# Modulation sums moved out of the feed-forward layers into the mixers of a fused transformer kernel

## The chip, the cores and the metric

The kernel runs as one program on one core of a Trainium2 chip. The metric is the device time of one execution in microseconds (us), the median of several runs. Of the core's engines, TensorE (PE) does the matmuls and writes PSUM, VectorE (DVE) and ScalarE (ACT) do the elementwise work, GpSimd (POOL) does a little, and SyncE (SP) issues most of the loads from HBM. ACT and POOL can issue loads too. Each engine works through its own list of instructions in order, and a wait on a semaphore holds everything behind it on that engine.

## The reference

Two blocks are computed one after the other on 256 tokens of width 1024, each with two layers, all in float32. A layer is a mixer (several kinds of token mixing side by side, then an output projection) and a feed-forward. The first block has one dense feed-forward and one with 8 experts, the second block has two dense ones. What matters here is the second block's modulation: a vector of 6 x 1024 numbers for each layer, from one conditioning vector `c`:

```python
c_act = jax.nn.silu(c)
for l in range(DEPTH):                                   # DEPTH = 2
    mod = (c_act @ ada_w[l] + ada_b[l])[:, None, :]      # ada_w[l]: 1024 x 6144
    sh1, sc1, g1, sh2, sc2, g2 = jnp.split(mod, 6, axis=-1)
    h = rmsnorm(x, norm_mix_g[l]) * (1.0 + sc1) + sh1
    ...                                                  # mixer, x = x + g1 * (mix @ w_out[l])
    h = rmsnorm(x, norm_ffn_g[l]) * (1.0 + sc2) + sh2
    f = (jax.nn.silu(h @ ffn_w1[l]) * (h @ ffn_w3[l])) @ ffn_w2[l]
    x = x + g2 * f
```

`mod` depends on nothing but the inputs, so it can be computed at any time before the layer that uses it.

## The kernel before, in words

The stages run in this order. First block: mixer 0 ("mix0"), dense feed-forward "ffn0", a gated projection "ple0", mixer 1 ("mix1"), the experts, "ple1". Second block: mixer "mixb0", feed-forward "ffnb0", mixer "mixb1", feed-forward "ffnb1", the final norm.

The order on every engine is written out by hand. Functions such as `dve_ff`, `act_mixers1` or `pe_mixers2` list the instructions of one engine for one stage, and every helper waits on named signals (`wait_ge`) and raises its own (`then_inc`). There is no scheduler. All compute instructions are issued in one helper line, which is why the profile gives L91 for nearly all of them, and L115 for the loads; they are told apart by engine and tile.

**The modulation sums.** `ada_w` comes as 48 chunks for each layer, each 128 rows by 1024 columns (512 KB). One DVE instruction (`dve_ada_sum`) multiplies a chunk by the replicated `c_act` (`c_row`) and sums along the row into one column of the tile `mods` ("modulation"). The chunk is loaded from the ACT queue (`act_ada_load`), each into one of four places of the big tile `ring`. The load into a place waits for the sum that read this place last (`adasum{n-4}`). The 48 chunks for layer 0 of the second block are all summed inside ffn0, and the 48 of layer 1 all inside ffnb0. Inside ffnb1 there are none. Both ffn0 and ffnb0 also load `c` and take its silu on ACT, at their start (`act_ada_start`).

**A feed-forward layer** has 22 blocks of 128 hidden columns, in 11 pairs. Pair 0 is done by plain matmuls (`pe_ff_up`). Pairs 1 to 10 use a Strassen-like scheme of seven products instead of eight (`pe_ff_pair`). For each of them DVE makes sums of weights for the next pair (`dve_ff_w`, 4 pieces), and puts the products together (`dve_ff_c11`, `dve_ff_c22`, `dve_ff_c12`, `dve_ff_pair_hid`); ACT copies one product and takes the silu. I call this the up stage. Then comes the down stage: 11 pairs of hidden blocks times the down weights, seven products of 128x512 each (`pe_ff_down`, n = 1, 2, 6, 5, 3, 7, 4), added up in seven PSUM banks. Product 6 of pair p waits for DVE: for the sums of hidden values (`dve_ff_hid_sums`, four instructions of 128x128) and of weights (`dve_ff_down_sums`, four of 128x512). PE runs pairs 0 to 7 one after the other, and the last three product by product, so that product 6 of pair 10 is its 65th of 77. At the end `dve_ff_close` adds the totals to the residual.

In `dve_ff` the modulation sums stand between these instructions: three in each of the pairs 1 to 10 of the up stage, one after it, and then one or two after each `dve_ff_down_sums`.

**The mixers.** PE goes through column tiles of the input projection (`pe_win`, 384 columns for 128 tokens at a time), ACT copies each result out of PSUM (`act_z`, written `z(t, i)`), and the next tile of the same half of the tokens waits for this copy. Between the tiles PE does the small matmuls of the mixing, in step with DVE and ACT. In mix1 DVE has nothing to do from the normalisation until `dve_rw_mix`, which needs the third tile, and then waits again before `dve_rw_wa`. In mixb0 it waits before `dve_cf_gate`, which starts a long chain of convolution taps, and again before the residual is added. The copies `act_rw_lo_copy` (mix1) and `act_cf_turn` (mixb0) stand between a turn on PE and what follows on PE or DVE.

SP loads the weights of the next stage into slots of `ring` as these come free. Some of those loads wait for the last modulation sum of the layer (`ada_done`).

Of the kernel before, what the change touches and what calls it, by code (L numbers as in the profile page):

```python
# [16 lines left out]
P = 128  # L17
# [218 lines left out]
def build(nc, d):  # L236
# [26 lines left out]
    mods = sb("modulation", 2 * 48 + 16)  # L263
    posi = nc.alloc_sbuf_tensor("posi", [P, 2 * NT], I32)[:, :]
# [1177 lines left out]
    SUMS_AT, TSUMS_AT, CGATE_AT, ADA_AT = (30720, 27648), 24576, 26624, (4096, 22528, 23552, 11264)  # L1442
    xs = xn_flat.rearrange("p (k t) -> p k t", k=KD)
    x_sums = flat[:, TSUMS_AT:TSUMS_AT + 2048].rearrange("p (e k t) -> p e k t", e=4, k=4)
    c_row = flat[:, CGATE_AT:CGATE_AT + D]
    ff_kept = xt_flat[:, 0:512]
    ADA_COLS = 48

# [323 lines left out]
    def act_ff(s, ada, l=None):  # L1772
        if ada is not None:
            act_ada_start(s, ada)
# [31 lines left out]
    def act_ada_load(s, ada, n):
        if n > 3:
            act.wait_ge(f"{s}.adasum{n - 4}")
        act.load(ada_place(n), d["ada"][ada, n], f"ada{n % 4}", f"{s}.ada{n}")

    def dve_ada_sum(s, ada, n):
# [3 lines left out]
        dve.wait_ge(f"{s}.ada{n}", f"{s}.crow")
        at = ADA_COLS * ada + n
        dve(V.scalar_tensor_tensor, out=ada_place(n), in0=ada_place(n), scalar=1.0, in1=c_row, op0=ALU.mult, op1=ALU.mult,
            accum_out=mods[:, at:at + 1]).then_inc(f"{s}.adasum{n}")

    def dve_ff(s, ada):  # L1820
        taken = iter(range(ADA_COLS if ada is not None else 0))

        def ada_sum():
            for n in itertools.islice(taken, 1):
                dve_ada_sum(s, ada, n)
# [11 lines left out]
        for p in range(1, NPAIR):  # L1837
# [5 lines left out]
            ada_sum()  # L1843
# [2351 lines left out]
```

## Time and profile before

| | us |
|---|---|
| runs | 2135.66, 2132.59, 2134.96 |
| median | 2134.96 |
| profiled execution, device time | 2133.81 |
| its span, first to last instruction | 2132.4 |
| PE busy in it | 2028.9 (95%) |
| DVE busy in it | 975.9 (46%) |
| ACT busy in it | 415.8 (20%) |

The granted TensorE clock is 0.983 of full speed over the span. The slices of the page show DVE at 8 or 9 tenths in two stretches only, which are ffn0 (about 206 to 438 us) and ffnb0 (about 1554 to 1788 us); in ffnb1 (about 1916 to 2121 us) it is at 6 or 7. PE is at 9 tenths nearly everywhere, and at 7 to 8 in some slices, two of which are the ends of ffn0 and ffnb0. A span counts as PE busy from the start of a matmul to its modelled end, so a PE that runs at half its clock also reads as busy.

### The profile page before, as it was taken

The page shows a single profiled execution, that of the slowest core. Times are in us where ns is not written, and L with a number is a line of the kernel's source. Part 1 is how long each engine was busy: PE and PEld are TensorE (multiplying, and loading weights), DVE is VectorE, ACT ScalarE, POOL GpSimd, SP SyncE. Part 2 cuts the span into 40 slices and gives each one's busy share as a digit, 9 for nine tenths or more (in the row PEclk, how much of TensorE's full clock was granted, in tenths as well). Part 3 has the DMA queues.
Part 4 walks back from the last instruction along what each step waited for, and adds up shares of the span by engine and source line. Part 5 has one row for each costly group of instructions (what it writes and reads, how often), then busy time and mean ns, then how long its engine had stood idle before and what let it go on. Part 6 is the DMA issues. An engine that isn't in the chain of part 4 may idle for free.

```text
span 2132.4 us, 31502 instructions
## 1 busy us (share of the span) xinstructions
PE 2028.9 (95%) x13197; PEld 1201.6 (56%) x13197; DVE 975.9 (46%) x1755; ACT 415.8 (20%) x918; POOL 60.8 (3%) x63
## 2 busy tenths in 40 slices
PE   8979999799988999999999999999999997999997
PEld 5665996365764433322333233366689834669973
DVE  2664899832773100000000000146579995747676
ACT  2454000031453000000101001052420002331001
POOL 0021000000110000000000000100000000000000
PEclk9999999899999999999999999999999999999999
DMA  6222977433233999999999999823378853435430
GB/s 236 92 111 117 364 289 271 150 153 118 82 130 127 405 423 414 416 424 410 423 412 424 424 424 424 356 112 139 138 296 299 295 166 131 159 139 231 174 139 30
DMA packets 70758, 536.54 MB, mean 252 GB/s; under 512 B 10129, under 2 KB 10641, under 8 KB 28529
## 3 DMA queue, kind: packets, MB, share of 16 engines
q1 hardware_dynamic: 53824, 474.28, 55.5%
q10 hardware_dynamic: 14112, 51.39, 6.8%
q0 software_dynamic: 2672, 8.78, 1.1%
q8 instruction: 107, 1.75, 0.3%
q14 instruction: 43, 0.34, 0.0%
HBM read 528.77 MB, written 7.75 MB: 252 GB/s over the span
## 4 chain that ended last, share of the span: by engine, by line
PE 67%; DVE 22%; DMA 6%; ACT 3%; issue 2%; DVEq 0%; SPq 0%; ACTq 0%
PE ps L91 67%; DVE ring L91 17%; DMA ring<-in_moe 6%; DVE transposed L91 2%; ACT ring L91 2%; DVE stat L91 1%; DVE natural L91 1%; DVE z L91 1%; ACT natural L91 1%; DVE gates L91 0%; DMA ring<-in_c 0%; DVE residual L91 0%; DVEq L75 0%; ACT L91 0%; ACT z L91 0%
## 5 line engine op out<-in xcount | busy, mean ns | idle before, releaser
L91 PE MATMUL ps<-ring 128*32 128x512 f32 (+8 forms) x5968 | 890.5, 446 | 62.8 <-DVE ring L91 45.0
L91 PEld LDWEIGHTS ps<-ring 128*128 128x128 f32 (+4 forms) x5968 | 472.0, 153 | 417.1 <-issue 335.1
L91 PE MATMUL ps<-ring,transposed 128*128 128x384 f32 (+4 forms) x1408 | 469.3, 489 | 3.3 <-ACT transposed L91 2.0
L91 PEld LDWEIGHTS ps<-ring,transposed 128*128 128x128 f32 x1408 | 259.4, 190 | 185.2 <-issue 62.2
L91 PE MATMUL ps<-ring,z 128*32 128x512 f32 (+4 forms) x1718 | 327.3, 581 | 0.3 <-ACT z L91 0.3
L91 DVE TENSOR_TENSOR z<-z,ps 128x256 f32<-128x256 f32 (+4 forms) x80 | 34.6, 433 | 622.9 <-ACT z L91 601.7
L91 DVE TENSOR_TENSOR ring<-ring 128x512 f32<-128x512 f32 (+3 forms) x320 | 275.8, 862 | 17.7 <-ACT ring L91 0.8
L91 PEld LDWEIGHTS ps<-ring,z 128*32 128x32 f32 (+3 forms) x1718 | 110.6, 129 | 195.5 <-issue 193.2
L91 DVE SCALAR_TENSOR_TENSOR ring<-ring 128x256 f32<-128x256 f32 (+3 forms) x222 | 177.0, 797 | 14.6
L91 PE MATMUL ps<-natural,ring 128*128 128x128 f32 (+1 forms) x1472 | 174.7, 275 | 1.4 <-ACT natural L91 0.8
L91 PEld LDWEIGHTS ps<-natural,ring 128*128 128x128 f32 x1472 | 169.5, 192 | 2.4 <-issue 1.2
L91 ACT COPY z<-ps 128x256 f32<-128x256 f32 (+6 forms) x112 | 46.9, 419 | 508.8 <-PE ps L91 508.1
L91 DVE TENSOR_TENSOR transposed<-transposed,ps 128x512 f32<-128x512 f32 (+1 forms) x120 | 74.5, 621 | 44.5 <-PE ps L91 36.2
L91 ACT ACTIVATE z<-transposed 128x512 f32<-128x512 f32 x30 | 18.9, 630 | 347.7 <-DVE transposed L91 347.7
L91 ACT ACT_TABLE_LOAD x59 | 75.7, 1283 | 16.1 <-issue 12.4
L91 ACT ACTIVATE z<-ps 128x256 f32<-128x256 f32 (+2 forms) x67 | 25.0, 373 | 215.3 <-PE ps L91 209.8
L91 ACT COPY transposed<-ps 128x256 f32<-128x256 f32 (+1 forms) x55 | 23.3, 424 | 188.9 <-PE ps L91 185.9
L91 ACT COPY ring<-ps 128x512 f32<-128x512 f32 (+4 forms) x80 | 41.5, 518 | 77.9 <-PE ps L91 74.8
L91 ACT ACTIVATE natural<-residual 128x512 f32<-128x512 f32 (+2 forms) x52 | 31.0, 597 | 123.4 <-DVE residual L91 115.5
L91 PEld LDWEIGHTS ps<-constants,z 128*128 128x128 f32 (+1 forms) x263 | 26.8, 146 | 49.8 <-issue 46.4
L91 ACT ACTIVATE z<-ps,stat 128x384 f32<-128x384 f32 (+2 forms) x44 | 24.4, 554 | 123.8 <-PE ps L91 122.7
L91 PE MATMUL ps<-transposed,ring 128*128 128x257 f32 (+2 forms) x208 | 43.8, 380 | 1.3 <-DVE transposed L91 1.3
(159 smaller groups left out, 1024.4 us busy)
## 6 DMA issues: line engine op xcount, KB each, us to landing
ring<-in_moe SPq DMA_DIRECT2D x87, 2048.0 KB, 20.1
ring<-in_moe SPq DMA_DIRECT2D x90, 1024.0 KB, 18.7
ring<-in_ffn_up SPq DMA_DIRECT2D x66, 1024.0 KB, 7.1
ring<-in_ada ACTq DMA_DIRECT2D x96, 512.0 KB, 4.4
ring<-in_w_in SPq DMA_DIRECT2D x25, 1536.0 KB, 6.4
ring<-in_ffn_down SPq DMA_DIRECT2D x33, 1024.0 KB, 7.2
ring<-in_w_out SPq DMA_DIRECT2D x12, 1536.0 KB, 7.1
ring<-in_ple_gate SPq DMA_DIRECT2D x4, 1536.0 KB, 11.8
```

Source lines behind the costliest of these rows:

```text
L91: self.ins = None if self.book.counting else op(*args, **kw)
```

## The change

The 96 sums and the 96 chunk loads stay. Their places change:

- A tile of its own, `ada_mem` ("ada_chunks", 3 x 1024 columns), holds two chunks and `c_row`. `c` is loaded and its silu taken once, in ffn0. The room in SBUF comes from a smaller scratch for GpSimd's DMA descriptors (`dynamic_dma_scratch_size=4096`).
- 33 of the 48 sums of layer 0 stay in ffn0. 15 go to mix1: 11 ahead of `dve_rw_mix` ("mix") and 4 ahead of `dve_rw_wa` ("wa"). 34 of layer 1 stay in ffnb0. 14 go to mixb0 ("mixb"): 9 ahead of `dve_cf_gate` and 5 ahead of the residual.
- In the up stage a pair has 3 or 2 sums in turn (`ADA_PAIRS`, 25 in all), in the down stage there is one for each pair (8 in ffn0, 9 in ffnb0).
- The sums and weights for down pair 0 (`dve_ff_hid_sums(s, 0)`, `dve_ff_down_sums(s, 0)`) are one step earlier on DVE, in all three dense layers.
- The loads go round over six places in the feed-forward, three in mix1 (two own ones and the end of `zbuf`), two for "wa", and five in mixb0. They are issued by ACT between its copies `z(t, i)`. A load waits for the sum that read the place before it.

```diff
+    ada_mem = sb("ada_chunks", 3 * D)
...
-    c_row = flat[:, CGATE_AT:CGATE_AT + D]
+    c_row = ada_mem[:, 2 * D:3 * D]
+    ADA_TURNS = {"ff": ("own0", "own1", "ring0", "ring1", "ring2", "ring3"), "mix": ("own0", "own1", "z"), "wa": ("own0", "own1"),
+                 "mixb": ("own0", "own1", "sums0", "sums1", "sums2")}
+    ADA_PAIRS = (3, 2, 3, 2, 3, 2, 3, 2, 3, 2)
+    ADA_PARTS = ([(0, "ff", sum(ADA_PAIRS) + 8), (0, "mix", 11), (0, "wa", 4)],
+                 [(1, "mixb", 14), (1, "ff", sum(ADA_PAIRS) + 9)])
...
     def act_ada_start(s, ada):
         act.part("ada")
         act.wait_ge(f"{s}.xt10", f"{s}.xt11")
-        act.load(c_row, d["c"].to_broadcast([P, D]), "c", f"{s}.c")
-        for n in range(4):
-            act_ada_load(s, ada, n)
-        act.wait_ge(f"{s}.c")
-        act(S.activation, c_row, c_row, ACT.Silu).then_inc(f"{s}.crow")
...
+        if ada == 0:
+            act.load(c_row, d["c"].to_broadcast([P, D]), "c", "ada.c")
+        for n in ada_of[ada, "ff"][:6]:
+            act_ada_load(n)
+        if ada == 0:
+            act.wait_ge("ada.c")
+            act(S.activation, c_row, c_row, ACT.Silu).then_inc("ada.crow")
+
+    def act_ada_load(n):
+        act.part("ada")
+        if ada_before[n] is not None:
+            act.wait_ge(f"ada.sum{ada_before[n]}")
+        act.load(ADA_SPOTS[ada_spot[n]], d["ada"][n // ADA_COLS, n % ADA_COLS], f"ada_{ada_spot[n]}", f"ada.chunk{n}")
...
@@ dve_ff, pairs of the up stage
             if more:
                 dve_ff_w(s, p + 1, 0)
-            ada_sum()
+            else:
+                dve_ff_hid_sums(s, 0)
+            ada_sums(1)
             if p > 1:
                 dve_ff_pair_hid(s, p - 1)
             if more:
                 dve_ff_w(s, p + 1, 1)
             else:
-                dve_ff_hid_sums(s, 0)
+                dve_ff_down_sums(s, 0)
             dve_ff_c11(s, p)
...
-            ada_sum()
+            ada_sums(1)
             dve_ff_c22(s, p)
             if more:
                 dve_ff_w(s, p + 1, 3)
-            else:
-                dve_ff_down_sums(s, 0)
-            ada_sum()
+            ada_sums(ADA_PAIRS[p - 1] - 2)
         dve_ff_c12(s, NPAIR - 1)
-        ada_sum()
         dve_ff_pair_hid(s, NPAIR - 1)
         for p in range(1, NPAIR):
             dve_ff_hid_sums(s, p)
             dve_ff_down_sums(s, p)
-            ada_sum()
-            if p % 5 != 0:
-                ada_sum()
+            ada_sums(1)
...
@@ act_mixers1
+        load_ada(3)
         z(0, 0)
+        load_ada(2)
         z(0, 1)
+        load_ada(2)
...
         z(1, 0)
+        load_ada(2)
         z(1, 1)
+        load_ada(2)
         z(2, 0)
         z(2, 1)
+        if l == 1:
+            for n in ada_of[0, "wa"][:2]:
+                act_ada_load(n)
         z(3, 0)
         z(3, 1)
         act_rw_lo(l)
+        if l == 1:
+            for n in ada_of[0, "wa"][2:]:
+                act_ada_load(n)
         z(4, 0)
@@ dve_mixers1
+        if l == 1:
+            for n in ada_of[0, "mix"]:
+                dve_ada_sum(n)
         dve_rw_mix(l, 0, 0)
...
         dve_rw_mix(l, 1, 1)
+        if l == 1:
+            for n in ada_of[0, "wa"]:
+                dve_ada_sum(n)
         dve_rw_wa(l)
@@ act_mixers2
+        load_ada(5)
         z(0, 0)
+        load_ada(2)
         z(0, 1)
+        load_ada(2)
         z(1, 0)
         z(1, 1)
         act_cf_gate(l)
         z(2, 0)
+        load_ada(5)
         act_cf_turn(l)
@@ dve_mixers2
+        if l == 0:
+            for n in ada_of[1, "mixb"][:9]:
+                dve_ada_sum(n)
         dve_cf_gate(l)
...
         dve_re_out(l)
+        if l == 0:
+            for n in ada_of[1, "mixb"][9:]:
+                dve_ada_sum(n)
...
-    nc = bacc.Bacc("TRN2", target_bir_lowering=False, num_devices=1)
+    nc = bacc.Bacc("TRN2", target_bir_lowering=False, num_devices=1, dynamic_dma_scratch_size=4096)
```

First place, DVE in the down stage of ffn0 (and, alike, of ffnb0). A pair is four instructions of 128x128 on the hidden values and one row of four of 128x512 on the weights; the instruction that writes `modulation` is a sum. Before:

```order
L91 TENSOR_TENSOR ring<-z 128x128
L91 TENSOR_TENSOR ring<-z,ring 128x128
L91 TENSOR_TENSOR ring<-ring 128x512 x4
L91 SCALAR_TENSOR_TENSOR ring,modulation<-ring 128x1024 x2
L91 TENSOR_TENSOR ring<-z 128x128
```

And now:

```order
L91 TENSOR_TENSOR ring<-z 128x128
L91 TENSOR_TENSOR ring<-z,ring 128x128
L91 TENSOR_TENSOR ring<-ring 128x512 x4
L91 SCALAR_TENSOR_TENSOR ring,modulation<-ring,ada_chunks 128x1024
L91 TENSOR_TENSOR ring<-z 128x128
```

One of the two sums of a pair is gone from this place (`ada_chunks` is named because `c_row` is read there now).

Second place, DVE in mix1, from the reciprocals of the normalisation to `dve_rw_wa` (`ring<-ps,ring 128x512 x2`); the rows of `ring<-ps,z` are `dve_rw_mix`. Before:

```order
L91 RECIPROCAL stat<-stat 128x1
L91 TENSOR_TENSOR ring<-ps,z 128x512
...
L91 TENSOR_TENSOR ring<-ring 128x512
L91 TENSOR_TENSOR ring<-ring,z 128x512
L91 TENSOR_TENSOR ring<-ps,ring 128x512 x2
```

And now:

```order
L91 RECIPROCAL stat<-stat 128x1
L91 SCALAR_TENSOR_TENSOR ada_chunks,modulation<-ada_chunks 128x1024 x2
L91 SCALAR_TENSOR_TENSOR z,modulation<-z,ada_chunks 128x1024
L91 SCALAR_TENSOR_TENSOR ada_chunks,modulation<-ada_chunks 128x1024 x2
...
L91 TENSOR_TENSOR ring<-ps,z 128x512
L91 TENSOR_TENSOR ring<-ring 128x512
L91 TENSOR_TENSOR ring<-ring,z 128x512
L91 SCALAR_TENSOR_TENSOR ada_chunks,modulation<-ada_chunks 128x1024 x4
L91 TENSOR_TENSOR ring<-ps,ring 128x512 x2
```

Eleven sums now stand ahead of `dve_rw_mix` and four ahead of `dve_rw_wa`, where there was nothing between.

Third place, ACT in mixb0, from the second tile's copies to the turned convolution input (`ring<-ps 128x2x256`, which is `act_cf_turn`). Before:

```order
L91 COPY z<-ps 128x384 x4
L91 ACT_TABLE_LOAD
L91 ACTIVATE ring<-z 128x512
L91 COPY z<-ps 128x384
L91 COPY ring<-ps 128x2x256
```

And now:

```order
L115 DMA ada_chunks<-in_ada 128x1024 x2
L115 DMA ring<-in_ada 128x1024 x3
L91 COPY z<-ps 128x384
L115 DMA ada_chunks<-in_ada 128x1024 x2
L91 COPY z<-ps 128x384
L115 DMA ring<-in_ada 128x1024 x2
L91 COPY z<-ps 128x384 x2
...
L115 DMA ring<-in_ada 128x1024
L115 DMA ada_chunks<-in_ada 128x1024 x2
L115 DMA ring<-in_ada 128x1024 x2
L91 COPY ring<-ps 128x2x256
```

Nine loads stand ahead of or between the first copies, and five directly ahead of `act_cf_turn`.

## Rows read from the trace of the kernel before

**Rows 1.** Page: chain that ended last, by engine; costliest group (busy, idle before).

```profile
PE 67%; DVE 22%; DMA 6%; ACT 3%; issue 2%; DVEq 0%; SPq 0%; ACTq 0%
...
L91 PE MATMUL ps<-ring 128*32 128x512 f32 (+8 forms) x5968 | 890.5, 446 | 62.8 <-DVE ring L91 45.0
```

**Rows 2.** Windows: length, PE, PEld, DVE, ACT, POOL busy, clock, DMA, GB/s.

```profile
346.28:437.75 91.47, 74.62 (x165) 31.22 (x163) 75.98 (x140) 4.74 (x10) 0.00 (x0) 0.91 0.52 187
1569.49:1696.31 126.82, 125.38 (x1121) 125.22 (x1121) 116.35 (x151) 10.30 (x21) 0.00 (x0) 1.00 0.80 299
1696.31:1788.16 91.85, 74.96 (x172) 31.95 (x170) 78.56 (x149) 5.32 (x12) 0.00 (x0) 0.91 0.55 189
1930.12:2055.18 125.06, 125.06 (x1121) 125.05 (x1120) 83.78 (x100) 9.88 (x20) 0.00 (x0) 1.00 0.44 169
2055.18:2121.27 66.09, 66.09 (x156) 29.08 (x154) 48.54 (x95) 4.74 (x10) 0.00 (x0) 1.00 0.15 56
```

**Rows 3.** Timeline of PE, down stages of ffn0 and ffnb0: start, us, [idle before].

```profile
352.08 5.37 PE L91 MATMUL ps<-ring 128*128 128x512 f32 x8 [3.92 <-DVE ring L91]
...
422.77 11.69 PE L91 MATMUL ps<-ring 128*128 128x512 f32 x20 [5.33 <-DVE ring L91]
434.30 1.04 PE L91 MATMUL ps<-constants,residual 128*128 128x128 f32 x8
...
1785.51 1.95 PE L91 MATMUL ps<-diagonal,residual 128*128 128x128 f32 x16
```

**Rows 4.** Timeline of DVE in ffn0: one pair up, one pair down.

```profile
251.80 0.69 DVE L91 TENSOR_TENSOR transposed<-transposed,ps 128x512 f32<-128x512 f32 x1
...
264.61 0.69 DVE L91 TENSOR_TENSOR transposed<-transposed,ps 128x512 f32<-128x512 f32 x1
...
374.55 1.23 DVE L91 SCALAR_TENSOR_TENSOR ring<-ring 128x1024 f32<-128x1024 f32 x1
...
375.89 1.23 DVE L91 SCALAR_TENSOR_TENSOR ring<-ring 128x1024 f32<-128x1024 f32 x1
...
381.58 1.23 DVE L91 SCALAR_TENSOR_TENSOR ring<-ring 128x1024 f32<-128x1024 f32 x1
```

**Rows 5.** Timeline of DVE in ffnb1: the sums for down pair 1.

```profile
2058.14 0.29 DVE L91 TENSOR_TENSOR ring<-z 128x128 f32<-128x128 f32 x1
```

**Rows 6.** Timelines of ACT and PE, start of ffnb0.

```profile
1555.66 2.02 ACTq L115 DMA_DIRECT2D ring<-in_ada  x4
1563.85 1.06 ACT L91 ACTIVATE ring<-ring 128x1024 f32<-128x1024 f32 x1 [4.80 <-DMA ring<-in_c]
...
1569.49 3.81 PE L91 MATMUL ps<-natural,ring 128*128 128x128 f32 x32 [0.83 <-ACT natural L91]
```

**Rows 7.** Chunk loads: all 96 by tile; then the four at 1555 us.

```profile
DMA to landing us min/median/max: 3.1/4.4/22.9
...
ring<-in_ada ACTq DMA_DIRECT2D x4, 512.0 KB, 17.4
```

**Rows 8.** Timelines of DVE, ACT and PE in mix1.

```profile
510.02 0.69 DVE L91 TENSOR_TENSOR ring<-ps,z 128x512 f32<-128x512 f32 x1 [28.54 <-PE ps L91]
...
525.95 0.42 ACT L91 ACTIVATE ring<-ring 128x256 f32<-128x256 f32 x1
531.09 0.69 DVE L91 TENSOR_TENSOR ring<-ps,ring 128x512 f32<-128x512 f32 x1 [9.47 <-PE ps L91]
...
551.60 2.00 PE L91 MATMUL ps<-natural,ring 128*128 128x64 f32 x16 [0.28 <-DVE natural L91]
```

**Rows 9.** Timelines of DVE, ACT and PE in mixb0.

```profile
1454.49 0.69 DVE L91 TENSOR_TENSOR ring<-ring,z 128x512 f32<-128x512 f32 x1 [17.44 <-ACT ring L91]
1457.79 0.59 ACT L91 COPY ring<-ps 128x512 f32<-128x512 f32 x1
1503.44 0.65 PE L91 MATMUL ps<-constants,ring 128*128 128x128 f32 x4 [0.26 <-DVE ring L91]
1542.65 0.69 DVE L91 TENSOR_TENSOR natural<-ps,gates 128x512 f32<-128x512 f32 x1 [15.32 <-PE ps L91]
```

More of the change, by code:

```diff
@@ L1772, in act_ff @@
     def act_ff(s, ada, l=None):
+        chunks = ada_of[ada, "ff"] if ada is not None else ()
         if ada is not None:
@@ L1783, in act_ff @@
             if ada is not None:
-                for n in range(3 * p + 1, 3 * p + 4):
-                    act_ada_load(s, ada, n)
+                more = 6 + sum(ADA_PAIRS[:p - 1])
+                for n in chunks[asked:more]:
+                    act_ada_load(n)
+                asked = more
         act_ff_silu_pair(s, NPAIR - 1)
-        if ada is not None:
-            for n in range(3 * NPAIR + 1, ADA_COLS):
-                act_ada_load(s, ada, n)
+        for n in chunks[asked:]:
+            act_ada_load(n)
         act.part("ff")
@@ L1799, in act_ada_start, with dve_ada_sum, ada_sums @@
         act.wait_ge(f"{s}.xt10", f"{s}.xt11")
-        act.load(c_row, d["c"].to_broadcast([P, D]), "c", f"{s}.c")
-        for n in range(4):
-            act_ada_load(s, ada, n)
-        act.wait_ge(f"{s}.c")
-        act(S.activation, c_row, c_row, ACT.Silu).then_inc(f"{s}.crow")
[L1806 to L1811, printed above, removed]
+        if ada == 0:
[10 more added lines that the diff above has]
+        act.load(ADA_SPOTS[ada_spot[n]], d["ada"][n // ADA_COLS, n % ADA_COLS], f"ada_{ada_spot[n]}", f"ada.chunk{n}")
+    def dve_ada_sum(n):
         dve.part("ada")
[L1815 to L1818, printed above, removed]
+        dve.wait_ge(f"ada.chunk{n}", "ada.crow")
+        at = ADA_SPOTS[ada_spot[n]]
+        dve(V.scalar_tensor_tensor, out=at, in0=at, scalar=1.0, in1=c_row, op0=ALU.mult, op1=ALU.mult,
+            accum_out=mods[:, n:n + 1]).then_inc(f"ada.sum{n}")
     def dve_ff(s, ada):
[L1821 to L1825, printed above, removed]
+        left = iter(ada_of[ada, "ff"] if ada is not None else ())
+        def ada_sums(count):
+            for n in itertools.islice(left, count):
+                dve_ada_sum(n)
         dve_row_scale(s)
@@ L3409, in act_mixers1, with load_ada @@
                 act_norm(s, i, "x{i}")
+        ada = iter([] if l == 0 else ada_of[0, "mix"])
+        def load_ada(count):
+            for n in itertools.islice(ada, count):
+                act_ada_load(n)
+        load_ada(3)
         z(0, 0)
+        load_ada(2)
         z(0, 1)
+        load_ada(2)
         if l == 0:
@@ L3686, in act_mixers2, with load_ada @@
         act_modulate_xt(s, 1, gains[:, 0:8], mod[:, 0:8])
+        ada = iter(ada_of[1, "mixb"] if l == 0 else [])
+        def load_ada(count):
+            for n in itertools.islice(ada, count):
+                act_ada_load(n)
+        load_ada(5)
         z(0, 0)
+        load_ada(2)
         z(0, 1)
+        load_ada(2)
         z(1, 0)
@@ L3844, in sp_program @@
         sp_ff("ffn0", d["ffn_up"], d["ffn_down"], 0, slots_after_mixers1(0))
-        ada_done = f"ffn0.adasum{ADA_COLS - 1}"
+        ada_done = f"ada.sum{ada_of[0, 'ff'][-1]}"
         after = [("ffn0.total4",), ("ffn0.down7", ada_done), ("ffn0.total4",), ("ffn0.total4", ada_done)] + [("ffn0.down5", ada_done)] * 4
@@ L3858, in sp_program @@
         sp_ff("ffnb0", d["ffn2_up"], d["ffn2_down"], 0, slots_after_mixers2(0))
-        after = [("ffnb0.down5", f"ffnb0.adasum{ADA_COLS - 1}")] * 4
+        after = [("ffnb0.down5", f"ada.sum{ada_of[1, 'ff'][-1]}")] * 4
         sp_mixers2(1, after)
```

20 lines of the change are left out of this document (17 added, 3 removed).

## Prediction

> **What bounds the kernel now.** I read the page first. The chain that ended last is 67% PE and 22% DVE, although the kernel is a matmul kernel, and the costliest group of matmuls stood idle 62.8 us, of which 45.0 ended with a DVE instruction on `ring` [rows 1]. So DVE holds PE back somewhere. The windows by stage show where. All three dense feed-forwards do the same matmuls, and ffnb1 alone has no modulation sums, so it is the measure for the other two. Its up stage (pairs 1 to 10) takes 125.06 us and its down stage 66.09, both with PE busy throughout and the clock at 1.00. The up stage of ffnb0 takes 126.82, but the down stages of ffn0 and ffnb0 take 91.47 and 91.85, at a mean clock of 0.91 [rows 2]. Hence the up stage is PE's and the loss is in the down stage. The timeline of PE there shows the waits for DVE, 3.92 us at the first pair and 5.33 at the last; eight matmuls that take 3.4 us in ffnb1's pace took 5.37 after the first of them [rows 3]. This is the second cost: after such a wait the granted clock falls to its lower level (1.2 GHz) for a while.
>
> Why DVE is late is in its own timeline [rows 4]. In the up stage the same instruction of two successive pairs starts at 251.80 and 264.61: 12.81 us of DVE work a pair, three sums included, against 12.51 on PE (125.06 / 10). DVE falls behind by 0.3 us a pair, which PE does not feel yet. In the down stage a pair with two sums takes 381.58 - 374.55 = 7.03 us, against 6.01 on PE (66.09 / 77 = 0.858 a product, 7 products). One sum costs 375.89 - 374.55 = 1.34.
>
> **The change part by part.** Sum and ranges go against the profiled execution, 2133.81 us, of which 2132.4 are its span; the median of the runs, 2134.96, lies 1.15 above it.
>
> *Up stages.* With 3 and 2 sums in turn DVE needs 12.81 and 11.47, on average 12.14, so it keeps pace with PE's 12.51. PE had no waits here, so this earns nothing by itself; what it earns is that DVE reaches the down stage on time.
>
> *Down stages.* I count from PE's first down product. The sums for pair 0 are now done in the pair before, under PE's 12.51 us. DVE can begin on pair 1 once the last silu is there, which was 2058.14 - 2055.18 = 2.96 us in ffnb1 [rows 5], where DVE came late from work that now stands earlier; I take 2.3. The four small and four large instructions take 7.03 - 2 x 1.34 = 4.35, so pair 1 is ready at 6.6. PE wants it at 6.01 + 2 x 0.858 = 7.7. From there DVE needs 4.35 + 1.34 = 5.69 a pair and PE 6.01, so DVE gains until PE's last group: product 6 of pair 10 is wanted after 64 products, at 54.9. DVE has it at 6.6 + 9 x 5.69 = 57.8 in ffnb0, and one sum earlier, at 56.5, in ffn0. Late by 2.9 and 1.6: these waits stay.
> ffn0 then takes 66.1 + 1.0 (the turn for ple0 that PE does in between [rows 3]) + 1.6 = 68.7 in place of 91.5: 22.8 gained. ffnb0 takes 66.1 + 1.9 (its turn [rows 3]) + 2.9 = 70.9 in place of 91.85: 20.9 gained. With 2.96 in place of 2.3, both waits grow by 0.7. If the 2.9 us wait drops the clock as the 3.92 did, it costs 5.37 - 3.4 = 2.0 more; none at all would give 4.5 back.
>
> *Start of ffnb0.* `c` isn't loaded a second time. ACT waited 4.80 us for it before its silu, which stood ahead of the bias that PE's pair 1 waits for (0.83) [rows 6]. With the 126.82 - 125.06 = 1.8 in the up stage [rows 2] this makes 2.6 gained; late next are ACT's six issues, 3 us from about 1555.7 (four took 2.02 [rows 6]), over ten microseconds before pair 1. In ffn0 `c` stays.
>
> *Mix1, eleven sums.* DVE is idle 28.54 us before 510.02, from 481.5 [rows 8]; 11 x 1.34 = 14.7 fit. They depend on their loads: three places, so four rounds of issue, landing and sum. The first three loads go out some 5 us before 481.5. Landing took 4.4 in the median [rows 7], so a round is about 4.4 + 1.3 + 0.5, and after a first sum at 482.8 three more rounds and a sum end near 503, under the cover. ACT is held by the loads' waits between its copies, but each has a whole tile of about 5 us to be late. I take 0; each microsecond of landing more moves the end by 4, and from about 6 on it shows.
>
> *Mix1, four sums.* DVE is idle 9.47 us before 531.09, and 4 x 1.34 = 5.4 would fit, but the last two loads are issued only behind `act_rw_lo`, after 525.95 + 0.42 = 526.4 [rows 8]. The third chunk lands at 530.8, is summed by 532.1, the fourth by 533.5: `dve_rw_wa` starts 2.5 late. Behind it DVE and ACT work nearly without a gap up to 551.60, where PE already waits for DVE [rows 8], so nothing absorbs it. 2.5 lost; with a landing of 3.1 it is 1.2, with the 17.4 of a crowded burst [rows 7] some 15.
> The Trainium skill, page "DMA: Bandwidth & Descriptors", section "Anatomy of one DMA", fits a transfer as about 2.0 us plus its bytes at 436 GB/s, 3.2 us for 512 KB; that is an estimate from the page. The fastest of the 96 loads agrees (3.1), the median doesn't. By the page the four sums would cost 1.3 in place of 2.5.
>
> *Mixb0, nine sums.* DVE is idle 17.44 us before 1454.49, from 1437.05 [rows 9]; 9 x 1.34 = 12.1 fit, in five places and so two rounds. With five issues of 0.5 ahead of the first copy, the ninth sum ends near 1454.7. 0, with up to 2 if landings are slower.
>
> *Mixb0, five loads.* They stand on ACT right ahead of `act_cf_turn`. All their waits are over by then, but 5 x 0.5 = 2.5 us of issuing delays the copy that starts the convolution on DVE, and DVE's chain runs on to PE's wait at 1503.44 [rows 9] with hardly a gap. 2.5 lost. The five sums of 6.7 lie in the 15.32 us before the residual [rows 9]: 0.
>
> *The smaller scratch for POOL's descriptors.* No row shows its use. POOL issues few transfers, all in the experts' stage; I take 0, with 0 to 3 as bounds.
>
> Sum: 22.8 + 20.9 + 2.6 - 2.5 - 2.5 = 41.3. The profiled execution becomes 2092.5, the median, 1.15 above, 2093.6.
>
> **Rivals.**
> A. *DVE stays behind in the down stage.* If it enters it some 3 us late, as its order makes it wait for PE's products in places where it now has little slack, the waits at pair 1 and at pair 10 grow by 3 in each layer, and each drops the clock once (2.0). For it: the margin at pair 1 is 7.7 - 6.6 = 1.1. Against: the mean of the up stage leaves 0.37 a pair to catch up. 2093.6 + 2 x (3 + 2) = 2104.
> Here the Trainium skill, page "TensorE: Matmul & The Clock Gate", section "What's actually happening", has the array fall to 1.2 GHz after it was idle and return only after sustained work. The traces agree for 3.92 us of idling (5.37 against 3.4); whether 2.9 suffices no row shows.
> B. *The mixers swallow everything*: landings near 3.1, and slack that I don't see takes the 2.5 us of issuing. 2093.6 - 5 = 2089. Against it speaks that PE waits for DVE already at 551.60 and 1503.44.
> C. *Slower: the loads hold the mixers.* If chunks land in the mixers as in the burst at 1555, 17.4 us, then mix1's first sums take four rounds of 19.2 from about 476 and end at 553 in place of 510 (43 lost), the "wa" ones cost 15, mixb0's two rounds of 19.2 and four more sums end at 1482 (27), with the issues 2.5: 88 against a gain of 46, 2176. These terms rise by about 7 us for each microsecond of landing, so it decides from about 11 us on. Against it: the 17.4 came while whole feed-forward blocks were being loaded, while in the mixers one tile of 1.5 MB comes in ten microseconds.
> D. *The change doesn't free PE*: once DVE is out of the way, something else sets the down stage, such as the down weights. It would keep perhaps half of the loss, 2093.6 + 22 = 2116. ffnb1 with the same loads and 66.09 speaks against it.
>
> **How the numbers follow.** My forecast has 0.67, its own range 2089 to 2100. A has 0.16, B 0.12, C 0.02, D 0.03. The range from 2086 to 2105 takes in A and B and leaves out C, D and the tails. What a measurement can tell from no change is 0.2%, 4 us. Only C is slower; D and a partial C could hardly come to rest within 4 us of 2135. Faster 0.97, same 0.01, slower 0.02.
>
> **What would show it.** Down stages of about 69 and 71 us at a clock of 1.00, with one PE wait for DVE in each, of 1.6 and 2.9, at the last pair; up stages of 125.1. No load of `c` in ffnb0 and no wait at pair 1. In mix1 DVE's first `ring<-ps,z` about as long after the start of PE's tiles as before, `dve_rw_wa` 2.5 us later, and PE waits for DVE between there and the matmul on `natural` that sum to about 2.5. In mixb0 five issues ahead of ACT's copy, and again about 2.5 us of PE waits by the place of 1503.44. I'm wrong if a down stage keeps waits at several pairs, if chunk loads in the mixers land in over 6 us, or if PE waits there for ACT's copies.

## Result and the profile after

The changed kernel takes 2098.4 us in the median of four runs (2097.59 to 2102.64), the kernel before beside it 2133.8 (2132.59 to 2135.66). The ratio is 0.9837, 95% interval [0.982, 0.9854]: faster by 1.6%. A second measurement gave 2096.1 (five runs, 2093.56 to 2103.13), ratio 0.983 [0.9814, 0.9846]. Forecast were 2093.6, between 2086 and 2105: right in sign and range, 4.8 us too low. The forecast's last step, 1.15 us from the profiled execution to the median, came from three runs of the kernel before; with the fourth their median is 2133.8 and equals the profiled 2133.81. In the spans, where the sum was made, the miss is 5.2 us (36.1 gained for 41.3).

The profiled execution took 2097.74 us, its span is 2096.3 (before 2132.4). From the page, the two lines that answer to [rows 1]: chain by engine, and the costliest group with its idle time.

```profile
PE 68%; DVE 21%; DMA 6%; ACT 3%; issue 2%; DVEq 0%; ACTq 0%; SPq 0%
...
L91 PE MATMUL ps<-ring 128*32 128x512 f32 (+8 forms) x5968 | 879.5, 444 | 33.8 <-DVE ring L91 15.3
```

PE's idle time ahead of this group fell from 62.8 to 33.8 us, the part that DVE ended from 45.0 to 15.3, and its busy time by 11 (the matmuls are the same, so they took less time each: more of them ran at the full clock). The windows answer to [rows 2]: up and down stage of ffn0, then of ffnb0 (length, PE, PEld, DVE, ACT, POOL busy, clock, DMA, GB/s).

```profile
222.42:347.48 125.06, 125.06 (x1122) 125.06 (x1120) 114.31 (x149) 9.78 (x20) 0.00 (x0) 1.00 0.79 304
347.48:418.96 71.48, 68.90 (x164) 30.57 (x163) 58.12 (x111) 4.74 (x10) 0.00 (x0) 0.98 0.39 151
1555.95:1681.01 125.06, 125.06 (x1122) 125.06 (x1120) 114.96 (x151) 9.88 (x20) 0.00 (x0) 1.00 0.75 291
1681.01:1752.43 71.42, 68.28 (x173) 30.81 (x171) 60.73 (x121) 5.65 (x12) 0.00 (x0) 1.00 0.40 157
```

Both up stages now take the 125.06 us of ffnb1, and the down stages 71.48 and 71.42. Each has one wait of PE for DVE left, at the last pair. PE's timeline (start, us, idle before) there, ffn0 and ffnb0:

```profile
405.16 10.52 PE L91 MATMUL ps<-ring 128*128 128x512 f32 x20 [2.58 <-DVE ring L91]
...
1739.06 8.82 PE L91 MATMUL ps<-ring 128*128 128x512 f32 x20 [2.95 <-DVE ring L91]
```

The same 20 matmuls took 10.52 us after the first wait and 8.82 after the second: in ffn0 the granted clock fell (I call this a dip), in ffnb0 not. Why the first wait is 2.58 stands in DVE's timeline: ffn0's down pair 1, its third sum, and for comparison pair 1 of ffnb0:

```profile
350.63 0.29 DVE L91 TENSOR_TENSOR ring<-z 128x128 f32<-128x128 f32 x1
...
366.65 1.23 DVE L91 SCALAR_TENSOR_TENSOR ring<-ring,ada_chunks 128x1024 f32<-128x1024 f32 x1 [0.47 <-DVE ring L91]
...
1683.56 0.29 DVE L91 TENSOR_TENSOR ring<-z 128x128 f32<-128x128 f32 x1
```

DVE begins on pair 1 at 350.63 - 347.48 = 3.15 us into the stage of ffn0, and once stands 0.47 more ahead of a sum. In ffnb0 it begins at 1683.56 - 1681.01 = 2.55 and never stands. The 0.47 is not a late chunk: the three loads issued from 339.37 on, of which this sum reads one, landed in 5.6 us in the median, and the same 0.47 stands at the same sum in nine of the ten profiles of the thinned kernels (all but e1), whatever the loads did. What it is the profiles don't show.

The mixers paid. In mix1, DVE's sums, then the `wa` step and what PE made of it, with the issue of the last two loads on ACT's queue (answering to [rows 8]):

```profile
477.29 1.22 DVE L91 SCALAR_TENSOR_TENSOR z<-z,ada_chunks 128x1024 f32<-128x1024 f32 x1 [6.38 <-DMA z<-in_ada]
...
491.23 0.69 DVE L91 TENSOR_TENSOR ring<-ps,z 128x512 f32<-128x512 f32 x1 [1.31 <-PE ps L91]
...
505.89 0.82 ACTq L115 DMA_DIRECT2D ada_chunks<-in_ada  x2
...
510.93 1.23 DVE L91 SCALAR_TENSOR_TENSOR ada_chunks<-ada_chunks 128x1024 f32<-128x1024 f32 x1 [5.42 <-DMA ada_chunks<-in_ada]
...
513.60 1.49 DVE L91 TENSOR_TENSOR ring<-ps,ring 128x512 f32<-128x512 f32 x2
...
534.06 2.00 PE L91 MATMUL ps<-natural,ring 128*128 128x64 f32 x16 [1.13 <-DVE natural L91]
```

The eleven sums are done in time, but only by 1.31 us: one chunk, issued at 467.16, took 10.1 us to land. Counted from PE's first tile (480.48 before, 461.69 now), `dve_rw_wa` starts at 51.91 in place of 50.61, so 1.3 us late. Behind PE's wait at 534.06 there is a dip: from there to the product on `constants` and `gates` at 546.26 it is 12.20 us, before 562.11 - 551.60 = 10.51, at a mean granted clock of 0.86 in place of 1.00. So mix1's loss is 1.3 us of waiting and 1.7 of clock. In mixb0 (answering to [rows 9]), DVE's gate, ACT's copy behind the five issues, and PE's waits:

```profile
1441.73 0.69 DVE L91 TENSOR_TENSOR ring<-ring,z 128x512 f32<-128x512 f32 x1
...
1442.48 0.65 PE L91 MATMUL ps<-constants,ring 128*128 128x128 f32 x4 [0.50 <-DVE ring L91]
...
1445.22 0.59 ACT L91 COPY ring<-ps 128x512 f32<-128x512 f32 x1 [2.73 <-issue]
...
1490.88 0.65 PE L91 MATMUL ps<-constants,ring 128*128 128x128 f32 x4 [1.47 <-DVE ring L91]
```

And the chunk loads of the whole kernel as the page groups them (KB each, median us to landing), against 4.4 before [rows 7]:

```profile
ring<-in_ada ACTq DMA_DIRECT2D x51, 512.0 KB, 6.0
ada_chunks<-in_ada ACTq DMA_DIRECT2D x42, 512.0 KB, 5.9
```

67 of these 96 loads are those of the feed-forwards. By stage the medians are 5.5 and 5.3 us in the up stages of ffn0 and ffnb0, 7.3 for the eleven loads issued from 457 to 481 us in mix1, and 8.8 for the first nine of mixb0 (9.5 at the most).

Where the 36.1 us of span went, cut at the same instruction in both executions:

| stretch | before | after | difference | forecast |
|---|---|---|---|---|
| start to ffn0's down stage | 346.28 | 347.48 | +1.2 | 0 |
| ffn0 down | 91.47 | 71.48 | -20.0 | -22.8 |
| ple0, mix1, experts, ple1, to mixb0's tiles | 999.15 | 1002.76 | +3.6 | +2.5 |
| mixb0 to PE's wait at 1503.44 / 1490.88 | 66.54 | 69.16 | +2.6 | +2.5 |
| from there to ffnb0's down stage | 192.87 | 190.13 | -2.7 | -2.6 |
| ffnb0 down, to the next stage's first matmul | 92.19 | 71.42 | -20.8 | -20.9 |
| the rest | 343.9 | 343.9 | 0.0 | 0 |

The sixth row ends 0.34 us later before than the window of [rows 2] (1788.50, not 1788.16). Against the 70.9 us that the prediction gave this stage, the 71.42 measured are 0.5 more.

### The profile page after: what moved, and what is told of

It reads as the page before. It is cut to its first block, busy times and chain, and to the rows that moved or that the text cites. A ratio compares the mean times of both kernels' runs of the same rounds, so it can differ in the third digit from the quotient of the medians.

```text
span 2096.3 us, 31499 instructions
## 1 busy us (share of the span) xinstructions
PE 2018.8 (96%) x13197; PEld 1200.8 (57%) x13197; DVE 976.0 (47%) x1755; ACT 414.8 (20%) x917; POOL 60.7 (3%) x63
## 4 chain that ended last, share of the span: by engine, by line
PE 68%; DVE 21%; DMA 6%; ACT 3%; issue 2%; DVEq 0%; ACTq 0%; SPq 0%
PE ps L91 68%; DVE ring L91 14%; DMA ring<-in_moe 6%; DVE transposed L91 2%; ACT ring L91 2%; DVE ada_chunks L91 1%; DVE stat L91 1%; DVE natural L91 1%; DVE z L91 1%; DVE gates L91 0%; ACT L91 0%; ACT natural L91 0%; ACT z L91 0%; DVE residual L91 0%; DVEq L75 0%
## 5 line engine op out<-in xcount | busy, mean ns | idle before, releaser
L91 PE MATMUL ps<-ring 128*32 128x512 f32 (+8 forms) x5968 | 879.5, 444 | 33.8 <-DVE ring L91 15.3
L91 DVE TENSOR_TENSOR transposed<-transposed,ps 128x512 f32<-128x512 f32 (+1 forms) x120 | 74.5, 621 | 44.8 <-PE ps L91 36.1
L91 DVE SCALAR_TENSOR_TENSOR ring<-ring,ada_chunks 128x1024 f32<-128x1024 f32 x51 | 62.5, 1225 | 8.2 <-DMA ring<-in_ada 2.7
L91 DVE SCALAR_TENSOR_TENSOR ring<-ring 128x256 f32<-128x256 f32 (+2 forms) x126 | 59.4, 472 | 4.5
L91 DVE SCALAR_TENSOR_TENSOR ada_chunks<-ada_chunks 128x1024 f32<-128x1024 f32 x42 | 51.5, 1225 | 16.4 <-DMA ada_chunks<-in_ada 12.7
```

The costliest lines, as they stand in the source:

```text
L91: self.ins = None if self.book.counting else op(*args, **kw)
```

## Experiments

Medians are of five runs or more; the kernel before took 2133.2 to 2134.2 beside each group of them.

**Theory:** the number of sums on DVE in the dense feed-forwards set the down stages, and the sums put into the mixers cost there what the loads (landings and issues) push back. **Rivals:** the gain came from the order at the turn to the down stage; the mixers' cost is only the spread between executions.

### All sums back, new order kept (e2_all_48_in_ffn)

```diff
-    ADA_PAIRS = (3, 2, 3, 2, 3, 2, 3, 2, 3, 2)
+    ADA_PAIRS = (3,) * 10
-    ADA_PARTS = ([(0, "ff", sum(ADA_PAIRS) + 8), (0, "mix", 11), (0, "wa", 4)],
-                 [(1, "mixb", 14), (1, "ff", sum(ADA_PAIRS) + 9)])
+    ADA_PARTS = ([(0, "ff", 48), (0, "mix", 0), (0, "wa", 0)],
+                 [(1, "mixb", 0), (1, "ff", 48)])
...
         dve_ff_c12(s, NPAIR - 1)
+        ada_sums(1)
...
-            ada_sums(1)
+            ada_sums(1 if p % 5 == 0 else 2)
```

> All 48 sums of each layer back in ffn0 and ffnb0, three a pair in the up stage and two in most down pairs as in the kernel before; the changed order on DVE (pair 0's sums one step earlier), the six buffers and the single load of c stay. Theory 1 (the number of sums on DVE sets the down stage): only c's 2.6 us and at most 1 us a layer for the order are kept, 2134 - 4 = 2130. Rival (the order at the turn to the down stage does half of the work): the waits at the first pair go, 2112. Down stages 90 us by theory 1, 80 by the rival.

Measured: 2130.66 (11 runs), ratio 0.9982 [0.9973, 0.9991]. PE's timeline in ffn0's down stage, its waits:

```profile
349.23 3.67 PE L91 MATMUL ps<-ring 128*128 128x512 f32 x8 [0.99 <-DVE ring L91]
...
361.18 6.65 PE L91 MATMUL ps<-ring 128*128 128x512 f32 x8 [5.70 <-DVE ring L91]
...
415.96 2.05 PE L91 MATMUL ps<-ring 128*128 128x512 f32 x2 [3.52 <-DVE ring L91]
423.34 11.44 PE L91 MATMUL ps<-ring 128*128 128x512 f32 x20 [5.33 <-DVE ring L91]
```

The waits have moved from the first pair to the second, and the stage is as long as before: from 346.36 to PE's `residual` product at 434.61 it is 88.25 us, before 434.30 - 346.28 = 88.02. Of the 3.5 us gained, 2.7 are the single load of `c`: from mixb0's convolution to ffnb0's down stage this kernel takes 190.13 us, as the changed one does (192.87 before), with all sums back. That leaves the order alone less than 1 us, and the thinning is the gain. It is the sums and not the relief of the DMA queues by fewer loads: in the kernel before, DVE itself waited for no load and no engine between 346.28 and 423, only once for 0.5 us behind an instruction of its own, while PE waited for DVE nine times in that stage, 16.8 us in all.

### The old order, sums thinned (e7_old_order)

```diff
                 dve_ff_w(s, p + 1, 0)
-            else:
-                dve_ff_hid_sums(s, 0)
             ada_sums(1)
...
             else:
-                dve_ff_down_sums(s, 0)
+                dve_ff_hid_sums(s, 0)
...
                 dve_ff_w(s, p + 1, 3)
+            else:
+                dve_ff_down_sums(s, 0)
```

> The changed kernel with DVE's old order at the turn to the down stage (pair 0's down operands behind the last up product's step in place of ahead of it), all sums where the changed kernel has them. Theory 1 (DVE's total is what ends the stage, since it has less slack there than PE): PE waits some 3 us at the first pair, which it then need not wait at the last, so the stage is as long and only the clock dips of two first waits are added, 2098.4 + 3 = 2101. Rival (the first wait adds in full, in both layers, and the last wait stays): 2098.4 + 2 x (3.9 + 2) = 2110. Other rival (the order doesn't matter at all): 2098.4 and no wait at the first pair.

Measured: 2103.61, ratio 0.985 [0.9837, 0.9864]. That is near the 2101 of theory 1, but its mechanism did not happen: PE does not wait at the first pair in either layer. What the profile shows is a last wait of 3.35 in ffnb0 (2.95 after) with a clock dip, and a stretch of mixb0, which the edit does not touch, in which the clock fell behind a wait of 1.46 us. Window (same columns as above) from that wait to the next stage's product, in this run:

```profile
1487.90:1505.72 17.82, 17.82 (x81) 14.10 (x81) 10.82 (x23) 7.89 (x16) 0.00 (x0) 0.71 0.00 1
```

After, the same stretch takes 1503.86 - 1490.88 = 12.98. These 4.8 us stand in one of four profiles with this code and this wait, so they are hardly the order's. But the profiled execution (2101.68) is the second fastest of the five, and what held the other three at 2103.61 to 2104.61 no profile shows. The interval overlaps those of both measurements of the changed kernel, yet all five runs lie above both of its medians, so the order may be worth nothing or up to some 5 us; this run doesn't settle it.

### The mixers' sums left out (e1_mixer_sums_out)

```diff
-            ada_of[l_, turns] = range(len(ada_spot), len(ada_spot) + count)
+            ada_of[l_, turns] = range(len(ada_spot), len(ada_spot) + (count if turns == "ff" else 0))
...
+            dve(V.memset, mods, 0.0)
```

> Left out: the 29 modulation sums of the three mixer places and their loads (15 in mix1, 14 in mixb0); those columns of the modulation are zero. What is left is the thinned feed-forwards. Theory 1 (the mixers pay what the profile after shows, 3.6 us in mix1 and 2.6 in mixb0): 2098.4 - 6.2 = 2092.2, the shift between the starts of ffn0's down stage and ffn1 as long as before. Rival (the profiled execution after was only unlucky there, the sums are hidden): 2097 to 2098.4. The down stages should not change (71.5 and 71.2), by either.

Measured: 2089.2, ratio 0.9785 [0.9772, 0.9799], 9.2 below the first measurement of the changed kernel and 6.9 below the second. Windows of mix1 (from its tiles to the second product on `gates` that waits) and of mixb0:

```profile
458.28:553.85 95.57, 94.11 (x521) 60.70 (x521) 42.55 (x84) 29.42 (x48) 6.82 (x7) 1.00 0.32 112
1414.19:1480.73 66.54, 66.29 (x281) 41.88 (x281) 40.15 (x91) 19.30 (x38) 0.00 (x0) 1.00 0.37 133
```

The same two windows of the changed kernel:

```profile
461.69:560.19 98.50, 96.07 (x520) 61.61 (x520) 61.08 (x114) 29.42 (x48) 6.81 (x7) 0.98 0.48 175
...
1421.72:1490.88 69.16, 66.75 (x280) 41.62 (x280) 51.26 (x109) 19.67 (x38) 0.00 (x0) 1.00 0.62 236
```

The kernel before takes 95.59 and 66.54 in these windows. 2.9 and 2.6 us are the mixers' cost in the profile after, so the rival falls: the cost stands in place and length where theory 1 has it. ffn0's last wait was 1.38 in this run, without a clock dip, although the expectation has the down stages unchanged; DVE began pair 1 at 349.28 - 346.96 = 2.32 us into the stage and had no wait of 0.47. ffnb0 went the other way: there DVE began at 2.93, the wait was 3.34, and the 20 matmuls behind it took 11.82 us. The edit touches neither, so a part of the 6.9 or 9.2 us is the spread of these two entries.

### Mix1's last two sums later (e4_mix1_two_sums_late)

```diff
-    ... (0, "wa", 4)],
+    ... (0, "wa", 2), (0, "late", 2)],
         act_rw_lo(l)
-        if l == 1:
-            for n in ada_of[0, "wa"][2:]:
-                act_ada_load(n)
...
         act_rw_hv(l)
+        if l == 1:
+            for n in ada_of[0, "late"]:
+                act_ada_load(n)
...
         dve_at_max(l, 5)
+        if l == 1:
+            for n in ada_of[0, "late"]:
+                dve_ada_sum(n)
```

> In mix1 only two sums stay ahead of the DVE step that waited for the last chunks (at 513.60 in the profile after); the other two are loaded some 85 us later and summed in DVE's idle stretch near 626. Theory 1 (the 5.42 us wait for the chunk cost 1.3 us, and PE's wait of 1.13 us that came of it dropped the clock for 1.3 us and more): 2098.4 - 3.3 = 2095.1 and no clock dip near 537. Rival A (only the 1.3 us, the dip has another cause): 2097.1. Rival B (the two sums stand in the way at the new place as well): 2098.4 or more.

Measured: 2093.65, ratio 0.9812 [0.9798, 0.9826]. Mix1's window, and PE's wait in the timeline:

```profile
459.12:554.76 95.64, 94.11 (x521) 60.80 (x521) 58.66 (x110) 29.40 (x48) 6.83 (x7) 1.00 0.46 169
```

```profile
530.24 2.00 PE L91 MATMUL ps<-natural,ring 128*128 128x64 f32 x16 [0.28 <-DVE natural L91]
```

The wait is 0.28 as before the change, and mix1 as short as without any sum (95.57). In this execution the eleven sums are hidden, and the last two of the four carried all of mix1's 2.9 us, the 1.7 of the dip among them.

### Mixb0: the five loads behind the copy (e3), and two chunks early as well (e10)

```diff
@@ act_mixers2
         z(2, 0)
-        load_ada(5)
         act_cf_turn(l)
         z(2, 1)
+        load_ada(2)
         z(3, 0)
+        load_ada(3)
```

> The five loads that stood on ACT ahead of the copy for the convolution are issued behind it, two after the next copy of z and three after the one behind that. Theory 1 (2.7 us of issuing delayed that copy and all that follows): 2098.4 - 2.5 = 2095.9, the PE wait of 1.47 us at 1490.88 back to about 0.3. Rival (the nine sums ahead of the gate are late anyway, 2.4 us, so that the copy isn't what ends last): 2098.4.

Measured: 2095.92, ratio 0.9823 [0.9807, 0.984]. The wait at 1490.88 was gone, but another had grown, and mixb0's window was longer than after (70.41 against 69.16):

```profile
1443.33 0.66 PE L91 MATMUL ps<-constants,ring 128*128 128x128 f32 x4 [2.14 <-DVE ring L91]
```

DVE's ninth sum stood 0.83 us for its chunk, others before it longer, and the gate came 21.66 us after PE's first tile (20.01 in the profile after, 17.59 in the kernel before), as the rival said. The time itself, 2095.92, is that of the changed kernel measured again (2096.12). Hence the next run, which adds this (the two early loads are taken from the front of the list):

```diff
         act_ple(1, 1)
+        for n in ada_of[1, "mixb"][:2]:
+            act_ada_load(n)
...
-        ada = iter(ada_of[1, "mixb"] if l == 0 else [])
+        ada = iter(ada_of[1, "mixb"][2:] if l == 0 else [])
...
-        load_ada(5)
+        load_ada(3)
         z(0, 0)
```

> The third run (five loads behind the copy) and the first two chunks of mixb0 loaded some 30 us earlier, in the stage before, so that DVE's nine sums begin at once. Theory 1 (mixb0 has two costs, one behind the other: the nine sums end late, 0.3 to 2.9 us by how the chunks land, and the issues hold the copy, 2.7; the larger one shows, which is why the third run gained less in its profile than its median said): both go, 2098.4 - 2.6 = 2095.8, from the start of mixb0's tiles to PE's fourth small product on `constants` and `ring` 66.5 us as in the kernel before, in place of 69.2 after and 70.4 in the third run. Rival (the loads behind the copy slow down something else there): 68 or more.

Measured: 2092.46, ratio 0.9811 [0.9798, 0.9825]. Window of mixb0, and in DVE's timeline its first sum and its gate:

```profile
1421.44:1487.97 66.53, 66.29 (x280) 41.96 (x280) 51.26 (x109) 19.27 (x38) 0.00 (x0) 1.00 0.60 228
```

```profile
1421.74 1.23 DVE L91 SCALAR_TENSOR_TENSOR ada_chunks<-ada_chunks 128x1024 f32<-128x1024 f32 x1
...
1439.03 0.69 DVE L91 TENSOR_TENSOR ring<-ring,z 128x512 f32<-128x512 f32 x1 [0.19 <-ACT ring L91]
```

66.53, the kernel before to 0.01. So mixb0 had two costs side by side, late sums and late issues, and the larger one shows; taking one away uncovers the other.

### Scratch alone on the kernel before (e8_scratch_alone)

```diff
-    ... num_devices=1)
+    ... num_devices=1, dynamic_dma_scratch_size=4096)
```

> The kernel before with nothing changed but the smaller scratch for descriptors. Theory 1: no effect, 2134. Rival (it holds back POOL's transfers in the experts' stage): 2135 to 2137, the experts' stage longer by as much.

Measured: 2135.06 (11 runs), ratio 1.0003 [0.9994, 1.0012]. No effect.

### The changed kernel again (e9_changed_again)

> The changed kernel itself, unchanged, a second time: 2098.4 again, within 1.5. What it is to show beside the time is which parts of the profile after are the kernel's and which that one execution's: the start of ffn0 (207 to 208), the last wait of ffn0's down stage with or without a clock dip, the PE wait ahead of mixb0's convolution (0.50 in the profile after, 0.30 to 2.85 in the runs that share its first nine sums).

Measured: 2096.12. ffn0's down stage has 2.69 of waiting with a dip; ffnb0's is this:

```profile
1735.70 10.48 PE L91 MATMUL ps<-ring 128*128 128x512 f32 x20 [2.95 <-DVE ring L91]
```

The same wait of 2.95 us of the same kernel, now with a dip. Ahead of the convolution's first product PE did not wait at all. Mix1's window was 559.02 - 461.18 = 97.84, 2.3 us above the 95.57 without sums, for other reasons than in the profile after. PE's wait between its tiles, and DVE's `wa` step:

```profile
477.67 13.17 PE L91 MATMUL ps<-ring,transposed 128*128 128x384 f32 x40 [0.74 <-DMA ring<-in_w_in]
...
514.11 1.49 DVE L91 TENSOR_TENSOR ring<-ps,ring 128x512 f32<-128x512 f32 x2
```

PE waited for a tile's weights, and DVE's first `dve_rw_mix` came 30.55 us after the first tile (29.54 in the kernel before and in the profile after), 1.0 late. `dve_rw_wa` came after 52.93, which is 2.3 late, so 1.3 are its own again, and no dip followed. In the five profiles with this mix1 code (after, e3, e7, e9, e10) the `wa` step's own delay is 1.3 to 1.6 us, two of them have the dip behind it (after and e10), and two a late tile (e3 0.5, e9 1.0). That the chunk loads made the tile late is likely (neither the kernel before nor e1, which lacks them, has this wait), but no run shows it.

### A faster version (e5, e6, e11)

e5 has the moves of e4 and e3.

> The five loads of mixb0 behind the copy for the convolution (as in the third run) and two sums of mix1 late (as in the fourth), together. They sit 900 us apart, so theory 1 has them add: 2098.4 - 2.5 - 4.8 = 2091.1. Rival (each gain was partly the spread between executions, some 3 us): 2094 or more.

Measured: 2092.61 (2087.9 to 2096.25), ratio 0.9804 [0.9791, 0.9818]: between theory and rival; e3's move alone leaves the late sums (a PE wait of 1.04 here). e6 then takes sums out of the down stages:

```diff
-    ... sum(ADA_PAIRS) + 8), ... (0, "late", 2)],
-                 [(1, "mixb", 14), (1, "ff", sum(ADA_PAIRS) + 9)])
+    ... sum(ADA_PAIRS) + 6), ... (0, "late", 2), (0, "adapt", 2)],
+                 [(1, "mixb", 16), (1, "ff", sum(ADA_PAIRS) + 7)])
```

> The fifth run, and two sums fewer in each down stage: in ffn0 (six in place of eight) the two are loaded behind the router and summed just ahead of the step that adds the modulation's rows; in ffnb0 (seven in place of nine) they follow the five in mixb0's idle stretch before the residual. Theory 1 (PE's last wait in each down stage is DVE's count of instructions and nothing else, 1.34 us a sum): the waits of 2.5 and 2.95 fall to 0 and 0.3, and no clock dip follows, 2091.1 - 2.5 - 2.7 - 1 = 2085. Rival (the last wait is set by how late DVE enters the stage, or the four sums cost as much at their new places): 2090 to 2092, with waits of over 2 us still there.

Measured: 2087.72, ratio 0.978 [0.9766, 0.9793]. PE's rows at the last pair of ffn0 and ffnb0:

```profile
400.05 10.46 PE L91 MATMUL ps<-ring 128*128 128x512 f32 x24
...
1732.16 8.82 PE L91 MATMUL ps<-ring 128*128 128x512 f32 x20 [0.93 <-DVE ring L91]
```

No wait in ffn0, and 2.0 less in ffnb0 for two sums (2.7 forecast; DVE began on pair 1 0.3 later). The 2085 us of the expectation were missed by the wait in mixb0, 2.85 in this run, and by a cost in the experts' stage that neither theory nor rival names. The two sums called "adapt" are loaded behind the router, and 60 us later PE waits longer for the experts' weights. PE there, in e11, which has the same two loads, and in the profile after:

```profile
720.57 6.12 PE L91 MATMUL ps<-ring 128*64 128x512 f32 x16 [5.54 <-DMA ring<-in_moe]
```

```profile
727.05 5.35 PE L91 MATMUL ps<-ring 128*64 128x512 f32 x16 [3.56 <-DMA ring<-in_moe]
```

In e6 the wait is 5.66; in the eleven profiles without the "adapt" loads it is 2.78 to 3.82. From the end of mix1's window to mixb0's first tile e6 and e11 take 864.1 and 864.2 us, the other eleven 859.3 to 861.7. So these two sums seem to cost about 2 us or more where they went, nearly what they gain in ffn0's down stage. No run moves them alone, so this is read from the profiles and not shown by an experiment.

e11 adds e10's early loads, ten sums in mixb0's first stretch and six in ffnb0's down stage.

> The sixth run, the two early loads of mixb0, a tenth sum in its first stretch and one sum fewer in ffnb0's down stage (six). Theory 1: PE's wait of 2.85 us in mixb0 and the last wait of 0.93 in ffnb0's down stage both go, 2087.7 - 2 - 0.9 = 2084.8. Rival (the tenth sum makes the ten late again): a PE wait of 1.3 us or more stays in mixb0, 2086.5.

Measured: 2086.22 (2085.43 to 2087.26), ratio 0.9777 [0.9764, 0.979]: no wait is left in either down stage, nor ahead of the convolution's first product (one of 0.63 is left where the changed kernel had 1.47). It beats the changed kernel by 10 us, and its five runs lie within 1.8 us where the changed kernel's second five span 9.6.

## Why the prediction was right, and where it was off

*The bound and the down stages: right.* DVE's count of instructions set them, with one wait left at the last pair. e2 shows that the thinning did it, e6 and e11 that the last wait goes with the sums. That ffnb0's wait came out as 2.95 for 2.9 is in part luck: DVE began on pair 1 at 2.55 and not at 2.3, and the arithmetic gives some 0.2 us too much (in e1 it began at 2.32, and ffn0's wait was 1.38 for 1.6).

*ffn0's last wait and its clock: the term mis-sized most, 2.8 of the 5.2 us that span and sum differ by.* Step "I take 2.3" for DVE's start on pair 1: it was 3.15, and 0.47 came on top, so the wait was 2.58 in place of 1.6. The row of ffnb1 had said 2.96; over all profiles of the thinned kernels the start, in either layer, lies between 2.3 and 3.3. The dip, which I priced at 2.0 and left out of the sum, came and cost 10.52 - 8.82 = 1.7.

*The first sums of mix1 at 0: right here, but not by the rule given.* I had written that from a landing of about 6 us on it shows. The median in this stretch was 7.3 and one load took 10.1, and yet 1.31 us were left. The prediction's own sign of being wrong, chunk loads in the mixers that land in over 6 us, came true. It cost nothing in mix1's first stretch, and it did in mixb0's.

*Mix1's four sums at 2.5: right place, half the size, and a total that is right by luck.* `dve_rw_wa` was 1.3 us late. I had the last two loads go out behind the whole of `act_rw_lo`, 45.9 us after PE's first tile (526.4 - 480.48); the trace has them at 505.89 - 461.69 = 44.2, while ACT is still at its last instructions, and a landing of 5.0 took back a part. The other 1.7 us of the 2.9 are the dip behind PE's wait of 1.13, which the sum doesn't have. e4 shows that both go with the last two sums. The further 0.7 us up to mixb0 are spread: in e9 the same stretch is 1.0 shorter than in the kernel before (859.82 against 860.83).

*Mixb0's nine sums at 0: wrong, and hidden by the next term.* They end 2.4 us late against the kernel before: their chunks took 8.8 us in the median, while DMA was busy 0.98 of the time. *The five issues at 2.5: right alone* (2.7 on ACT). The two delays overlap, so the total of 2.6 came out right with one term wrong, which is luck. e3 against e10 shows this. PE's wait of 0.44 for ACT at 1484.44, which the profile after, e7 and e9 have, was the third sign that I had named; it went with the five issues (none in e3 and e10).

*`c` once: 2.7 against 2.6.* e2 keeps it with all sums back and has the same 190.13 us. *Scratch: 0*, e8.

*Start +1.2.* The code up to there is the same; PE's last product ahead of ffn0 starts between 205.76 and 207.76 in thirteen profiles, with and without the change. It is spread.

*Rivals.* Of A a small part came: DVE entered ffn0's down stage 0.85 us later than I took, not 3, and one dip followed. B, mixers without a cost, is not this kernel; e4 and e10 had to move loads for it. C would decide from 11 us of landing on; the worst in mix1's first stretch was 10.1 and in e9 11.2, once each. D falls with e11, whose down stages have no wait left.

*The two pages.* Chunks took 5.9 and 6.0 us in the median in the changed kernel. The estimate of 3.2 us from the Trainium skill, page "DMA: Bandwidth & Descriptors", section "Anatomy of one DMA", is met by the fastest alone (3.2). The 1.3 us that the prediction drew from it for the four sums are what was measured, but with a landing of 5.0 and earlier issues, so not for its reason. In mixb0's first stretch DMA was busy 0.98 of the time, and that fit of the Trainium skill is measured on GpSimd's path, while these loads go by ACT's queue beside SyncE's.

```profile
1422.28:1441.73 19.45, 19.45 (x62) 11.27 (x60) 11.10 (x18) 4.28 (x7) 0.00 (x0) 1.00 0.98 387
```

On the clock, which the Trainium skill, page "TensorE: Matmul & The Clock Gate", section "What's actually happening", has fall after idling, the open question whether 2.9 us suffices has no single answer here; see below.

## What to carry to other kernels

Where a helper engine holds back the main one in a short stage, count the helper's instructions for each step against the time the main engine needs for it. Move optional work into an idle stretch only if the loads that it needs also land within it, and take their landing times from a stretch where the queues are as busy as there. Issue such loads before the stretch begins, and not right ahead of an instruction that starts a chain. When two delays overlap, removing one proves nothing: take both away before judging either. Where work goes, look at the whole kernel again; where two loads were put at a quiet place of ACT, PE waited longer for other weights 60 us later.

## What the runs showed that I had not expected

- The same wait of 2.95 us at the same matmul left the granted clock alone in the profile after (20 matmuls in 8.82 us) and dropped it in the second profile of the same kernel (10.48, mean granted clock 0.84 in that window, that is partly 1.2 GHz). Over all profiles of the thinned kernels, last waits of 0.93, 1.38, 2.30, 2.43, 2.87 and 2.93 had no dip, while 2.40, 2.55, 2.58, 2.69, 3.34 and 3.35 had one: the length of the wait alone does not tell. A dip cost 1.5 to 1.7 us, once 3.0 (11.82, after 3.34).
- The clock can fall behind a wait of only 1.46 us (e7, 0.71 over 17.82 us, 4.8 us lost), where three other profiles (1.47, 1.39 and 1.46) kept 1.00 behind the same wait.
- The times of the changed kernel go with its mean granted clock: in e9's five executions 2093.56 us has 0.992, the three from 2096.04 to 2096.49 have 0.990 and 0.991, and 2103.13 has 0.987. In e11 the clock goes from 0.988 to 0.992 as well, and the time only from 2087.26 to 2085.43.
- Landing of 512 KB on ACT's queue: 4.4 us in the median before, 7.3 beside mix1's tile loads and 8.8 beside those of mixb0, with 10.1 at the worst in mix1.
